# Expert layer of a hybrid block: the down bias added by VectorE where it takes a block from PSUM, instead of being mixed into the first sums in DRAM

## The reference

```python
top_v, top_i = lax.top_k(logits, TOP_K)              # 4 of 32
gates = jax.nn.softmax(top_v, axis=-1)
# assignments sorted by expert into blocks that hold one expert only
def expert_block(args):
    xblk, e = args
    gu = xblk @ w_gu[e] + b_gu[e]
    gate = jnp.minimum(gu[:, ::2], SWIGLU_LIMIT)
    up = jnp.clip(gu[:, 1::2], -SWIGLU_LIMIT, SWIGLU_LIMIT)
    act = (up + 1.0) * gate * jax.nn.sigmoid(SWIGLU_ALPHA * gate)
    return act @ w_down[e] + b_down[e]
...
return jnp.zeros_like(h).at[tok_sorted].add(y * gate)  # each row back to its token
x = x + mod * rmsnorm(that)
```

## Time and profile before

| | us |
|---|---|
| median of 3 executions | 2664.91 |
| lowest, highest | 2655.5, 2669.05 |
| the profiled execution: time | 2674.82 |
| its span, from the first to the last instruction | 2673.0 |
| PE busy in it | 2431.1 (91%) |
| DVE busy in it | 1805.6 (68%) |
| ACT busy in it | 1556.7 (58%) |

### The profile page before, as it was taken

One profiled execution on the slowest core, in us unless ns is written; L12 is line 12 of the kernel. 1 busy time (PEld: TensorE's weight loads), 2 busy tenths in 40 slices (PEclk: granted clock), 3 DMA queues, 4 the chain that ended last, 5 costly groups with the idle time before them and its releaser, 6 DMA issues. The chain is left out here.

```text
span 2673.0 us, 135770 instructions
## 1 busy us (share of the span) xinstructions
PE 2431.1 (91%) x57165; PEld 2153.8 (81%) x57165; DVE 1805.6 (68%) x2119; ACT 1556.7 (58%) x1972; POOL 808.7 (30%) x638
## 2 busy tenths in 40 slices
PE   6999998999988759999899989988889999999993
PEld 2455558999984449989898989988888999999993
DVE  3786986666657772552818377777877686788883
ACT  4524544555555352553737467777776676677873
POOL 3222116767731121221212232222222222223230
PEclk9999998999999869999999999999999999999996
DMA  8621001101122283572919397889988797899965
GB/s 286 242 77 62 1 16 35 31 24 31 31 91 80 95 331 95 170 258 56 372 33 371 121 337 261 309 315 345 334 300 315 283 321 253 285 330 369 330 244 195
DMA packets 123432, 536.91 MB, mean 201 GB/s; under 512 B 12236, under 2 KB 12608, under 8 KB 90560
## 3 DMA queue, kind: packets, MB, share of 16 engines
q1 hardware_dynamic: 107120, 481.80, 48.2%
q0 software_dynamic: 14880, 48.91, 8.2%
q10 hardware_dynamic: 1360, 5.24, 0.5%
HBM read 496.99 MB, written 38.92 MB: 200 GB/s over the span
## 5 line engine op out<-in xcount | busy, mean ns | idle before, releaser
L2523 PE MATMUL ps<-qkv,weights 128*128 128x64 f16 x10496 | 938.2, 193 | 68.0 <-DVE weights L1937 34.1
L2523 PEld LDWEIGHTS ps<-qkv,weights 128*128 128x128 f16 x10496 | 922.0, 98 | 85.4 <-DVE weights L1937 40.0
L2525 PE MATMUL ps<-qkv,weights 128*128 128x64 f16 x10496 | 937.8, 193 | 4.9 <-issue 4.9
L2524 PE MATMUL ps<-qkv,weights 128*128 128x64 f16 x10496 | 937.8, 193 | 0.1
L2525 PEld LDWEIGHTS ps<-qkv,weights 128*128 128x128 f16 x10496 | 922.5, 98 | 2.4 <-issue 2.4
L2524 PEld LDWEIGHTS ps<-qkv,weights 128*128 128x128 f16 x10496 | 922.5, 98 | 0.2 <-issue 0.2
L1937 DVE SCALAR_TENSOR_TENSOR weights<-hT,weights 128x2048 f16<-128x2048 f16 (+1 forms) x256 | 587.8, 2346 | 167.4 <-ACT weights L1320 138.1
L1320 ACT ACTIVATE weights<-hT 128x2048 f16 (+1 forms) x256 | 527.1, 2101 | 87.1 <-DMA hT<-in_w_gu_dram 65.4
L2540 PE MATMUL ps<-qkv,weights 128*128 128x64 f16 x5248 | 472.8, 193 | 24.6 <-DVE weights L1942 22.3
L2540 PEld LDWEIGHTS ps<-qkv,weights 128*128 128x128 f16 x5248 | 461.7, 98 | 32.3 <-DVE weights L1942 27.9
L2541 PE MATMUL ps<-qkv,weights 128*128 128x64 f16 x5248 | 472.5, 193 | 0.0
(11 more groups left out here) (450 smaller groups left out, 4308.2 us busy)
## 6 DMA issues: line engine op xcount, KB each, us to landing
hT<-in_w_gu_dram SPq DMA_DIRECT2D x256, 1024.0 KB, 8.6
qkv<-in_w_down_dram SPq DMA_DIRECT2D x128, 1024.0 KB, 6.2
weights<-in_w_ada_dram SPq DMA_DIRECT2D x8, 2048.0 KB, 14.4
qkv<-in_w_in_dram SPq DMA_DIRECT2D x4, 2048.0 KB, 9.0
qkv<-in_w_ada_dram SPq DMA_DIRECT2D x4, 2048.0 KB, 8.7
hT<-decay_rows SPq DMA_DIRECT2D x20, 256.0 KB, 3.3
hT<-beta_rows SPq DMA_DIRECT2D x20, 256.0 KB, 3.3
qkv<-in_x_dram ACTq DMA_DIRECT2D x4, 1024.0 KB, 8.1
```

Source lines behind the costliest of these rows:

```text
L2523: pe.matmul(dst, ghi[k][:, b, c], xT[:, 0, k, :], start=first, stop=False, skip_group_check=True)
L2524: pe.matmul(dst, ghi[k][:, b, c], xT[:, 1, k, :], start=False, stop=False, skip_group_check=True)
L2525: last = pe.matmul(dst, glo[k][:, b, c], xT[:, 0, k, :], start=False, stop=end, skip_group_check=True)
```

## The change

`b_down` is loaded once. PE turns it (eight transposes of 32 rows, one for each 128 columns), and ACT copies the result (128x256) over the constants `ones` and `iota`, which nothing reads any more by then; eight neighbouring columns of that tile are one expert's bias. The copy of a block's down sums out of PSUM goes from ACT to DVE, and becomes one instruction that multiplies by a constant and adds those eight columns, each held over 64 rows. Where the next block begins a new expert it stands behind the first of the four low down halves; otherwise where `next_down` does nothing else. `y_scratch` is filled with zeros by two 2 MB DMAs of SP, ahead of the DeltaNet's later chunks, and all that made the first sums is gone.

```diff
+        bdT = sb("ones_and_iota_then_b_down", [P, NE * KD])
+        ones, iota = bdT[:, 0:P], bdT[:, P:2 * P]
...
             for s in range(1, NC):
                 load_rows(s, False)
-            sp.wait_ge(s_zero, 33)
+            for i in range(2):
+                sp.dma_start(y_d[i * SEQ // 2:(i + 1) * SEQ // 2, :].rearrange("(p r) d -> p (r d)", p=P),
+                             slot(5)).then_inc(s_zero, 16)
+            sp.wait_ge(s_zero, 65)
...
-            sp.wait_ge(s_bd, NT)
+            sp.wait_ge(s_bdT, 1)
             down_chunk(e, 3)
...
             gather(0)
-            for n in range(6):
-                store_y_start(n)
             gather(1)
-            for n in range(6, NT):
-                store_y_start(n)
...
-            for n in range(4):
-                copy_y_start(n)
-            token_one_hots(0)
-            token_one_hots(1)
-            copy_y_start(4)
-            token_one_hots(2)
-            token_one_hots(3)
-            for k in range(3):
+            for q in range(4):
+                token_one_hots(q)
+            act.wait_ge(s_bdT, 1)
+            act.activation(bdT[:].rearrange("p (e c) -> p c e", e=NE), ps[:, 2, 0:NE * KD].rearrange("p (c e) -> p c e", c=KD),
+                           ACT.Copy).then_inc(s_bdT, 1)
+            for k in range(4):
                 high_gate_up(0, 0, k)
-            copy_y_start(5)
-            high_gate_up(0, 0, 3)
-            copy_y_start(6)
             copy_xT(0)
             name_rows(1)
-            high_gate_up(0, 0, 4)
-            copy_y_start(7)
-            for k in range(5, GK):
+            for k in range(4, GK):
                 high_gate_up(0, 0, k)
-            act.wait_ge(s_yin[0], 16 * 5)
...
                     high_act(t + 1)
-                    copy_yT(t)
                     scale_y(t - 1)
...
+            def copy_yT(t, e):
+                dve.wait_ge(s_dn, t * DK + 2 * DK)
+                reached(dve, s_ty, t, 1, EMPTY)
+                dve.scalar_tensor_tensor(yT, ps[:, BT, :].rearrange("p (c t) -> p c t", c=8), 1.0 / (ALPHA * WSCALE * WSCALE),
+                                         bdT[:, bass.ds(e * 8, 8)].unsqueeze(2).to_broadcast([P, 8, B]), ALU.mult,
+                                         ALU.add).then_inc(s_yT, 1)
+
-            def next_down(t, new, r):
+            def next_down(t, new, r, e):
                 with dve.If(new > 0):
-                    for j in range(DK):
+                    low_down(r, 0)
+                    copy_yT(t - 1, e)
+                    for j in range(1, DK):
                         low_down(r, j)
                 with dve.Else():
                     dve.wait_ge(s_dlo, t * DK + DK)
                     dve.sem_inc(s_dlo, DK)
+                    copy_yT(t - 1, e)
```

88 lines of the change are left out of this document (13 added, 75 removed).

## The result

| | before, as unchanged in the same session | changed |
|---|---|---|
| median, us | 2658.59 | 2671.27 |
| lowest, highest (8 executions each) | 2654.92, 2669.05 | 2670.35, 2678.47 |
| profiled execution: time (span) | 2674.82 (2673.0) | 2671.16 (2669.4) |

That is under the 0.5% (13.3 us) that the prediction took as the least that can be told from no change, and it is inside the range; but the interval leaves out 1, and a gain of 2.8 us was forecast. The two profiled executions stand the other way round, 3.7 us in favour of the change: that of before is one of its slowest. The reader should take totals from the timed runs, and only the places and the waits from the traces.

A forecast was written before the change was run, and what follows sets the result against it. PE was taken to bound the expert loop, and busy DMA engines the stretch ahead. Start -8, loop copy +5.1 and rest +0.1 sum to -2.8 us: 2662.1 by the median, range 2650 to 2675 (chance 0.82).

The forecast's parts named there:

- Part 1: Start of the experts: removing the first sums gains time; -8 us, from -1.5 to -14.3.
- room on the DMA engines: Loads of expert 0: without the first sums' stores the eighth chunk comes earlier, near 978; 7 us taken.
- gap of 5.18 us: Ahead of block 1: it starts 5.18 us behind, after block 0's SwiGLU, and this gap moves along whole.
- Part 2: Expert loop: the copy on DVE costs +5.1 us, from 0 to +12.5; +1.8 of it in nine pairs.
- +0.7 in three such experts: Late two-block experts: copy inserted in DVE's chain, 2.1 us in three; six others at 0.2 each, 1.2.
- Part 3: DVE's register load for the expert's number, each loop iteration: 0; exposed in all 82, 25 us.
- Part 4: SP's zeros, 4.2 MB issued about 430, ahead of the row loads: 0 taken, from 0 to +2 us.
- Part 5: The rest: `b_down` halves and router instruction 0, the last copy at the end +0.1 us.
- B: Rival, chance 0.17: start gives little, by DVE's pace or block 1's gap, loop costs as summed; +3.7, 2668.6 us.
- D: Rival, chance 0.09: at expert changes DVE's copy waits for PE's down, delaying low halves; 2710, or 2678 without added wait.
- E: Rival, chance 0.04: the bias load and its register are on the path; +22, so 2687 us.
- a longer wait of PE's `turn_y`: Sign of being wrong: PE's `turn_y` waits longer for DVE's new copy instruction; no size given.

The follow-up runs named there:

- `a_start`: Changed kernel plus 34 unread signals in PE's program, the copy back on ACT in its old place without bias: 0.9974 of the kernel before, -6.9 us.
- `b_loop`: Kernel before with the copy on DVE adding a column of zeros, no register load, first sums kept: 1.0037 of the kernel before, +9.9 us.
- `a_small`: Changed kernel plus 34 unread signals in PE's program, DVE copying only 8 of a block's 64 rows: 0.9996 of the kernel before.
- `a_ahead`: Changed kernel plus 34 unread signals in PE's program, the copy ahead of the first low down half: 1.0085 of the kernel before.

## Why the prediction was wrong in its sign

The sum said -8 + 5.1 + 0.1 = -2.8. The runs say -6.9 for `a_start`, +8.5 for the loop and +8.8 for the head. These three add up to the +10.4 measured by the way that they are taken, as differences along one chain of kernels; an independent check is `b_loop` alone, with +9.9 for the loop.

- **Part 1, the start: right in sign, its size in part by luck.** `a_start` has -6.9 against -8, but only some 4 to 5 us of it show at the start, and the rest in a loop whose code did not change. Its largest step, room on the DMA engines, was taken as 7: in the traces the eighth chunk's high half comes 3.5 us earlier behind the table, and 4.4 in all, at 980.97 and not at 978. The one-hots and the table came 1.1 earlier (26.1 us from DVE's one-hots to the table became 25.0) where 1.5 was taken. Block 1 began at 997.62 and not near 993. The prediction reads its gap of 5.18 us as standing behind the SwiGLU of block 0 and lets it move along whole. That reading is wrong: DVE had read block 0's gate/up by 996.08 and ACT had copied the turned rows by 996.71, and PE's sequencer was in its jump from 994.64 to 999.86. In the changed kernel the jump took 5.68 us and the gap 6.27, with the stall at the head in it.
- **Part 2, the copy in the loop: mis-sized.** Its duration was right (0.690 against 0.69), and the sum for the pairs (+1.8) is not contradicted (in the traces 0.4 to 2.4 over `a_start`, -0.7 to 5.4 with the block behind them), although the mechanism differed: PE's wait for the low halves fell, and `turn_y` took it up. The step that failed is "+0.7 in three such experts" and "in six others" 0.2, where I had counted as DVE's limit only those with one pattern of waits. In the traces the nine late blocks lose 5 to 8 us together where 3.3 was taken, 0.5 to 0.9 in each on the mean. `a_small` shows that this isn't DVE's chain alone (187.6 us with a copy of 0.22). The total of 8.5 to 9.9 lies inside the bound of 12.5.
- **No term for PE's own program.** This is the step that was missing. I took PE's side of "the first sums are gone" as a pure gain; but with 34 instructions fewer ahead of it the loop's head lies elsewhere, and that costs 8.8 us. Without it, what I did price measured +1.6 (-6.9 + 8.5), which no run tells from nothing. The Trainium skill, "Runtime: NRT & Kernel Launch", section "Instruction fetch mechanics", has an engine's program fetched in blocks, calls the cost of crossing from one to the next "mostly hidden", and says that a taken branch to a target outside the blocks that are held has to wait for a fetch. If the stall is such a crossing, it is not hidden right behind a jump back: 0.23 us in 80 passes. The long jump in the first iteration (4.1 to 6.3 us) fits the page's sentence on branches. That either is a fetch is the page's reading; the runs show only that the stall has a fixed place in the program, and that the jump is long once.
- **Part 3, the register load: right.** 309 ns at the median, not exposed. **Part 4, the zeros: right.** They are issued at 430.5, and SP's row loads, DVE's router and its one-hots behind them come within 0.4 us of those of before. **Part 5** is too small to see.
- **The rivals.** None is what happened. B's time (2668.6) is the nearest by number. Its cause, a start that gives little, is not what `a_start` has (-6.9), though the jump ahead of block 1 did take up a little of it (5.68 us for 5.21). D did not occur in the changed kernel and does in `a_ahead`. E is out by the register load's row and by `b_loop`.
- **The signs to look for.** DVE's read of gate/up waits 68 us less for PE, not 40; 106.8 us of waiting has gone to the copy, which in ordinary blocks holds up nothing. The sign "a longer wait of PE's `turn_y`" was named as one of being wrong, and it did come, yet it replaced a wait of the same size.

## What to carry to other kernels

When an edit takes instructions out ahead of a loop, compare the "issue" gap at the loop's head before and after, and shift the head by a few instructions before judging the edit; here one instruction more or less was worth 0.33%. Where two engines are both full around an event, work moved from one to the other comes back as a wait; count for each such place which engine ends last, all of them, and not those with the clearest pattern. Compare two traces at the same place of the work, not at the same time, and take a group of blocks wide enough to hold the block in which a delay comes out. And split a change into its parts early: a gain of 6.9 and two losses near 9 looked like one small loss.

## What the runs showed of the hardware that was not expected

- A fixed place in PE's program costs it 0.22 to 0.23 us in each pass if it lies between the first four instructions behind the jump back (290 or 276 ns in place of 58), and nothing that shows when the loop's head is on it or clear of it.
- PE's first jump over 200 matmuls with their weight loads took it 4.1 to 6.3 us in fourteen traces; the profile puts the gap down to "issue" or to another engine's sequencer (DVEq in the earlier trace rows), and only the branch's own duration shows it.
- Small activations on ACT from PSUM with a column as bias follow each other every 0.216 us (1.72 for eight, 128x64); on DVE the form with a broadcast column takes 0.69 us for 128x512 and the next instruction starts 0.60 to 0.61 after it (2431.84 to 2432.45).
- Executions of the same instructions reach the experts up to 6 us apart (954.40 and 960.16), and a granted clock of 1.00 or 0.91 in one stretch of 40 us goes with it roughly; what sets it is not shown.
